# A two-block transformer kernel on Trainium2: raw tokens transposed, first weights in pieces, the second attention's norms moved, halves of features at each handover

## The reference

```python
h = rms_norm(x, norm_mix[l])                      # x * rsqrt(mean(x*x) + 1e-6), then * gain
proj = jnp.einsum('btd,de->bte', h, w_in[l])      # 1024 -> 4352
q_a, k_a, v_a, q_b, k_b, v_b, g_a, g_b = jnp.split(proj, IN_SPLITS, axis=-1)
q_a = rms_norm(q_a.reshape(B, T, NA_HEADS, HEAD_DIM), q_norm_a[l])
k_a = rms_norm(k_a.reshape(B, T, NA_HEADS, HEAD_DIM), k_norm_a[l])
o_a = neighbourhood_attention(q_a, k_a, v_a, rpb_a[l]).reshape(B, T, A_W)
q_b = rms_norm(q_b.reshape(B, T, SW_HEADS, HEAD_DIM), q_norm_b[l])
k_b = rms_norm(k_b.reshape(B, T, SW_KV_HEADS, HEAD_DIM), k_norm_b[l])
o_b = sliding_window_attention(q_b, k_b, v_b, sink_b[l], t5_table).reshape(B, T, B_QW)
y = (jax.nn.sigmoid(g_a) * jnp.einsum('bte,ed->btd', o_a, w_branch_a[l])
     + jax.nn.sigmoid(g_b) * jnp.einsum('bte,ed->btd', o_b, w_branch_b[l]))
x = x + jnp.einsum('btd,de->bte', y, w_out[l])
h = rms_norm(x, norm_ffn[l])
u = jax.nn.silu(jnp.einsum('btd,df->btf', h, w_gate[l])) * jnp.einsum('btd,df->btf', h, w_up[l])
x = x + jnp.einsum('btf,fd->btd', u, w_down[l])
```

## Time and profile before

| | |
|---|---|
| median of 3 runs | 1085.29 us (1083.16 to 1090.6) |
| the profiled execution | 1087.0 us |
| its span from first to last instruction | 1085.2 us |
| TensorE busy | 920.6 us, 85% |
| VectorE busy | 444.6 us, 41% |
| ScalarE busy | 317.4 us, 29% |
| moved by DMA | 294.90 MB, mean 272 GB/s |
| mean granted TensorE clock | 0.949 |

### The profile page before, as it was taken

How to read it: one execution, slowest core, us unless ns; L and a number is a source line. 1 busy time by engine, 2 the same in 40 slices (tenths; PEclk the granted TensorE clock), 3 DMA queues, 4 the chain that set the end, 5 groups by cost and what they waited for, 6 DMA issues and landing times.

```text
span 1085.2 us, 18086 instructions
## 1 busy us (share of the span) xinstructions
PE 920.6 (85%) x7830; PEld 653.7 (60%) x7830; DVE 444.6 (41%) x556; ACT 317.4 (29%) x400; POOL 19.0 (2%) x36
## 2 busy tenths in 40 slices
PE   5989998999999998999988978776867768677875
PEld 5989987899999888999977823131313113131311
DVE  4576778466565438995766501010101000010102
ACT  5346674273443418554433300000000000000001
POOL 1300000000000000000000100000000000000000
PEclk9998999999999999999998998898989899998988
DMA  9993244336555445352035889999999999999994
GB/s 340 263 331 106 80 155 155 122 128 209 164 179 210 160 154 212 134 195 79 4 120 199 325 347 422 420 422 422 422 422 422 422 422 422 422 422 422 422 422 174
DMA packets 83396, 294.90 MB, mean 272 GB/s; under 512 B 5888, under 2 KB 33168, under 8 KB 58625
## 3 DMA queue, kind: packets, MB, share of 16 engines
q1 hardware_dynamic: 78240, 284.18, 67.4%
q10 hardware_dynamic: 3552, 6.07, 1.6%
q0 software_dynamic: 1536, 3.68, 1.3%
HBM read 290.76 MB, written 4.10 MB: 272 GB/s over the span
## 4 chain that ended last, share of the span: by engine, by line
PE 52%; DMA 36%; DVE 6%; SPq 2%; issue 2%; ACT 2%; DVEq 0%; ACTq 0%
DMA arena<-in_w_down 19%; DMA arena<-in_w_up 16%; PE psum L929 13%; PE psum L930 13%; PE psum L931 13%; PE psum L1230 3%; PE psum L1433 3%; SPq L790 2%; DVE ring_rounded L1888 1%; PE psum L904 1%; PE psum L896 1%; PE psum L1453 1%; PE psum L1002 1%; PE psum L1422 1%; PE psum L1480 1%
## 5 line engine op out<-in xcount | busy, mean ns | idle before, releaser
L1433 PE MATMUL psum<-arena,featL 128*32 128x512 f32 x1024 | 181.1, 681 | 64.2 <-DMA arena<-in_w_up 47.5
L1888 DVE TENSOR_TENSOR ring_rounded<-arena,hi_rounded 128x2048 fp32r<-128x2048 f32 x77 | 176.0, 2289 | 96.2 <-ACT hi_rounded L1535 95.2
L1535 ACT ACTIVATE hi_rounded<-arena 128x2048 fp32r<-128x2048 f32 x77 | 146.8, 1912 | 164.6 <-PE psum L931 55.8
L929 PE MATMUL psum<-hi_rounded,featT_rounded 128*128 128x256 f32 (+1 forms) x560 | 167.6, 299 | 10.0 <-DVE featL_rounded L1911 5.4
L930 PE MATMUL psum<-ring_rounded,featT_rounded 128*128 128x256 f32 (+1 forms) x560 | 165.5, 296 | 0.0
L931 PE MATMUL psum<-hi_rounded,featL_rounded 128*128 128x256 f32 (+1 forms) x560 | 165.3, 295 | 0.0
L1433 PEld LDWEIGHTS psum<-arena,featL 128*32 128x32 f32 x1024 | 40.2, 121 | 198.4 <-DMA arena<-in_w_up 88.3
L1453 PE MATMUL psum<-arena 128*32 128x512 f32 x512 | 95.7, 673 | 45.6 <-DMA arena<-in_w_down 39.8
L929 PEld LDWEIGHTS psum<-hi_rounded,featT_rounded 128*128 128x128 f32 x560 | 111.2, 199 | 13.3 <-DVE featL_rounded L1911 6.0
L930 PEld LDWEIGHTS psum<-ring_rounded,featT_rounded 128*128 128x128 f32 x560 | 111.3, 199 | 1.2
L931 PEld LDWEIGHTS psum<-hi_rounded,featL_rounded 128*128 128x128 f32 x560 | 111.1, 198 | 1.3
(11 more groups left out here) (279 smaller groups left out, 1137.0 us busy)
## 6 DMA issues: line engine op xcount, KB each, us to landing
arena<-in_w_gate SPq DMA_DIRECT2D x75, 1024.0 KB, 26.5
arena<-in_w_up SPq DMA_DIRECT2D x75, 1024.0 KB, 26.6
arena<-in_w_down SPq DMA_DIRECT2D x65, 1024.0 KB, 26.7
arena<-in_w_in SPq DMA_DIRECT2D x14, 2048.0 KB, 8.8
arena<-in_w_down SPq DMA_DIRECT2D x5, 2048.0 KB, 7.8
arena<-in_w_out SPq DMA_DIRECT2D x4, 2048.0 KB, 8.3
arena<-in_w_in SPq DMA_DIRECT2D x4, 1024.0 KB, 9.5
t_copies<-arena ACTq DMA_DIRECT2D x1, 2048.0 KB, 7.6
```

The source lines that it names most:

```text
L929: mm(o, lhs[0], rhs[0], start=start, stop=False, skip_group_check=True)
L1433: ins = mm(psum[32 * j:32 * j + 32, MB[4 + m], :], xg[:, 4 * half + k, 32 * j:32 * j + 32], quad[quad_slot(q)][:, j, 512 * k:512 * k + 512 ...
L1535: fn(high, view, ACT.Copy).then_inc(hi_ready, 1)
L1888: tt(low, view, high.bitcast(F32), ALU.subtract).then_inc(lo_ready, 1)
```

## The change

- The tokens are transposed as they are, without the norm. The two halves of the features take turns, each with its own gain, rounding and remainder. The factor of the norm, one for each token, is applied when ScalarE empties the projections (`scaled`), which is now two instructions, one for each tile of tokens. The squares and roots come behind the roundings of chunk 0 in ScalarE's program and ahead of that of chunk 1.
- The half of the first weight unit that holds chunk 0 is loaded by four DMAs of two row blocks each, and rounded and subtracted in four pieces (`first_high`, in `norm_T` of VectorE); `first_project` waits for each piece.
- TensorE multiplies zeros ahead of and behind the first transposes (`awake`, 16 and 10 matmuls).
- The matmul of `t5` stands behind unit 3 instead of unit 2.
- Squares and sums for `qb` and `kb` stand in VectorE's step 0 behind the remainder of chunk 10, root in ScalarE's step 0, scaling in VectorE's step 1 ahead of `weighted(0)`, transposes and copies in step 2. `kdup` and the temporary lie in `xn`.
- `y`: the first half of the features is transposed and split behind each tile of the second branch, both first weight remainders of `wo` come ahead of the last two tiles, and the first chunk of `wo` is multiplied in two halves of features, the last group's transposes between them.
- `features` with `lows` does the first six row blocks for both halves of the chunk, and then the last two.

Left out below: the same moves in `plan_fills`, the definitions of semaphores, `kdup`, and the split of the norms' loop into `qk_squares` and `qk_scaled`, which hold the same instructions as before.

```diff
                     off, k, w, src = parts[0]
-                    for h in range(2):
-                        cols_ = slice(w // 2 * h, w // 2 * (h + 1))
-                        nc.sync.dma_start(piece(off, k, w)[:, :, cols_], src[:, :, cols_]).then_inc((first_in, slot_in[0])[h], 16)
+                    for j in range(4):
+                        nc.sync.dma_start(piece(off, k, w)[:, 2 * j:2 * j + 2, 0:w // 2], src[:, 2 * j:2 * j + 2, 0:w // 2])\
+                            .then_inc(first_in[j], 16)
+                    nc.sync.dma_start(piece(off, k, w)[:, :, w // 2:w], src[:, :, w // 2:w]).then_inc(slot_in[0], 16)
...
             def norm_T():
-                for t in range(NT):
-                    for h in range(2):
-                        transposes(("nt", 0, t, h), [xn[:, t, (4 * h + k) * P:(4 * h + k + 1) * P] for k in range(4)],
-                                   lambda: pe.wait_ge(xn_ready, t + 1))
+                for h in range(2):
+                    for t in range(NT):
+                        transposes(("nt", 0, t, h), [x[:, t, (4 * h + k) * P:(4 * h + k + 1) * P] for k in range(4)],
+                                   lambda: pe.wait_ge(x_in[t], 16))
...
+            def first_project():
+                b = begin("p1", 0, 0).rearrange("p (t n) -> p t n", t=NT)
+                for j in range(4):
+                    if j < 3:
+                        pe.wait_ge(first_lo, j + 1)
+                    else:
+                        wait_split(pe, 0)
+                    for t in range(NT):
+                        pe.wait_ge(feat_lo, 2 * (j // 2) + t + 1)
+                        ins = project_tile(b, 0, t, range(2 * j, 2 * j + 2), fresh=j + t == 0)
                 end(ins)
...
             def features(key, name, c, feats, lows=None):
...
                 wait_split(pe, g)
-                for f in range(2):
-                    for k in range(DK):
-                        if lows is not None and f == 0 and k % 2 == 0:
-                            pe.wait_ge(feat_lo, lows + k // 2 + 1)
-                        ins = mm3(b[:, f, :], [part(g, k, P * f, P) for part in (hi_cols, lo_cols)],
-                                  [r[:, k, :] for r in feats], k == 0, k == DK - 1)
+                for ks in (range(DK),) if lows is None else (range(0, 6), range(6, DK)):
+                    for f in range(2):
+                        for k in ks:
+                            if lows is not None and f == 0 and k % 2 == 0:
+                                pe.wait_ge(feat_lo, lows + k // 2 + 1)
+                            ins = mm3(b[:, f, :], [part(g, k, P * f, P) for part in (hi_cols, lo_cols)],
+                                      [r[:, k, :] for r in feats], k == 0 and (f == 0 or lows is None), k == DK - 1)
                 end(ins)
...
+            def awake(n):
+                for _ in range(n):
+                    mm(psum[:, 7, 0:P], rt[:, 512:512 + P], rt[:, 512:512 + P], start=True, stop=True)
+            pe.wait_ge(blank_ready, 1)
+            awake(16)
             pe.wait_ge(ident_in, 32)
             norm_T()
+            awake(10)
...
-                    project(("p1", u, c), ("p1", u), c, first=u + c == 0)
-                if u == 2:
+                    if u + c == 0:
+                        first_project()
+                    else:
+                        project(("p1", u, c), ("p1", u), c)
+                if u == 3:
...
                     scores(i)
                 if i >= 1:
                     turned(i - 1)
-                if i == 0:
-                    turn_qk("qb", "kb")
                 if i < 8:
                     u, c = 5 + i // 2, i % 2
                     project(("p1", u, c), ("p1", u), c)
+                if i == 2:
+                    turn_qk("qb", "kb")
                 if i == 8:
                     for key in ((0, 0), (0, 1), (1, 0)):
                         turn_out(*key)
                 if i >= 1:
                     weighted(i - 1)
+            def turn_y(t, h, b=None):
+                b = (begin("yT", t, h) if b is None else b).rearrange("p (k q) -> p k q", q=P)
+                pe.wait_ge(y_ready, 2 * h + t + 1)
+                for k in range(4):
+                    ins = tr(b[:, k, :], sig[:, t, (4 * h + k) * P:(4 * h + k + 1) * P], ident)
+                end(ins)
...
-            for h in range(2):
-                for t in range(NT):
-                    transposes(("yT", t, h), [sig[:, t, (4 * h + k) * P:(4 * h + k + 1) * P] for k in range(4)],
-                               lambda: pe.wait_ge(y_ready, 2 * h + t + 1))
-            wait_emptied(pe, "yT", 1, 1)
+                        if br and n:
+                            turn_y(t, 0)
+            turn_y(0, 1)
+            last_T = begin("yT", 1, 1)
+            b = begin("wo", 0, 0).rearrange("p (t n) -> p t n", t=NT)
+            g = chunk_of[("wo", 0), 0]
+            wait_split(pe, g)
+            for t in range(NT):
+                wait_emptied(pe, "yT", t, 0)
+                project_tile(b, g, t, range(DK // 2), fresh=t == 0)
+            turn_y(1, 1, last_T)
+            for t in range(NT):
+                wait_emptied(pe, "yT", t, 1)
+                ins = project_tile(b, g, t, range(DK // 2, DK), fresh=False)
+            end(ins)
...
-                fn(warm[:], eps_col[:, 0:1], ACT.Sqrt)
+                if n:
+                    fn(warm[:], eps_col[:, 0:1], ACT.Sqrt)
...
-            def high_features():
+            def high_features(h):
...
                 for t in range(NT):
-                    for h in range(2):
-                        wait_emptied(act, "nt", 0, t, h)
-                        fn(featR[:, 4 * h:4 * h + 4, t * P:(t + 1) * P],
-                           featL[:, 4 * h:4 * h + 4, t * P:(t + 1) * P], ACT.Copy).then_inc(feat_hi, 1)
+                    wait_emptied(act, "nt", 0, t, h)
+                    fn(featR[:, 4 * h:4 * h + 4, t * P:(t + 1) * P],
+                       featL[:, 4 * h:4 * h + 4, t * P:(t + 1) * P], ACT.Copy).then_inc(feat_hi, 1)
...
+            def first_high(j):
+                high, view, _ = hi_view(0)
+                act.wait_ge(first_in[j], 16)
+                fn(high[:, 2 * j:2 * j + 2], view[:, 2 * j:2 * j + 2], ACT.Copy).then_inc(first_hi if j < 3 else hi_ready, 1)
...
             act.wait_ge(eps_ready, 3)
+            fn(warm[:], eps_col[:, 0:1], ACT.Sqrt)
+            high_features(0)
+            for j in range(2):
+                first_high(j)
+            high_features(1)
+            for j in range(2, 4):
+                first_high(j)
             squares(0, lambda t: act.wait_ge(x_in[t], 16))
-            high_part(0)
-            high_features()
             high_part(1)
...
+            def scaled(dst, lo, u, c):
+                b = bank("p1", u, c).rearrange("p (t n) -> p t n", t=NT)
+                a.link(fn(dst[:, 0, lo:lo + 256], b[:, 0, :], ACT.Copy, scale=st[:, 0:1]))
+                empty(fn(dst[:, 1, lo:lo + 256], b[:, 1, :], ACT.Copy, scale=st[:, 1:2]), "p1", u, c)
             act.wait_ge(ident_in, 32)
+            act.wait_ge(scale0_ready, NT)
...
-                empty(fn(nat[:, :, lo:lo + 256], bank("p1", u, c).rearrange("p (t n) -> p t n", t=NT), ACT.Copy), "p1", u, c)
-                if n == 5:
+                scaled(nat, lo, u, c)
+                if n == 7:
                     wait_filled(act, "t5")
...
-            root(*QK_SUMS[1], HD, 0)
...
-                if i == 0:
-                    qk_moved("qb", "kb")
...
-                    ins = fn(sig[:, :, 256 * i:256 * i + 256], bank("p1", u, c).rearrange("p (t n) -> p t n", t=NT), ACT.Copy)
-                    empty(ins, "p1", u, c)
+                    scaled(sig, 256 * i, u, c)
                     high_part(first["p1", 5] + i + 2)
+                    if i == 0:
+                        root(*QK_SUMS[1], HD, 0)
+                    if i == 2:
+                        qk_moved("qb", "kb")
...
+                _, whole, rounded = hi_view(0)
+                high0 = hi_view(0)[0]
+                for h in range(2):
+                    for t in range(NT):
+                        wait_filled(dve, "nt", 0, t, h)
+                        gain = bc(colp("norm0")[:, 4 * h:4 * h + 4], P)
+                        empty(tt(view(featL, t, h), bank("nt", 0, t, h).rearrange("p (k q) -> p k q", k=4), gain, ALU.mult),
+                              "nt", 0, t, h)
+                    for t in range(NT):
+                        highs[0] += 1
+                        dve.wait_ge(feat_hi, highs[0])
+                        tt(view(featLR, t, h), view(featL, t, h), view(featR, t, h).bitcast(F32), ALU.subtract).then_inc(feat_lo, 1)
+                    for j in (2 * h, 2 * h + 1):
+                        ks = slice(2 * j, 2 * j + 2)
+                        if j < 3:
+                            dve.wait_ge(first_hi, j + 1)
+                        else:
+                            dve.wait_ge(hi_ready, 1)
```

(28 more changed lines are left out.)

93 lines of the change are left out of this document (41 added, 52 removed).

## The result

| | before | after |
|---|---|---|
| median | 1085.79 us (1083.13 to 1090.8, 20 runs) | 1091.36 us (1087.56 to 1094.82, 20 runs) |
| span of the profiled execution | 1085.2 us | 1090.0 us |

The ratio is 1.0047, with a 95% interval of 1.0033 to 1.0061: the change makes the kernel about 5 us slower. That is inside the forecast range (1082.5 to 1094.0) and 2.5 us above the predicted 1088.9.

What follows compares the result with a forecast made beforehand. Before 225 us TensorE's waits, mostly for VectorE's operands, shift everything behind them, with no slack. Start and bias matmul +3.5, Part 4 +4.4, Part 5 -4.3 give +3.6: 1088.9 us on the median, range 1082.5 to 1094.0.

Steps and rivals of the forecast that it cites:

- Part 1: Start, first projection chunks: TensorE waits ahead of chunks 1 and 2, and chunk 2 ends 5.1 us later.
- Rival (a): Start: the DMA issues run through once delayed, chunk 2 starts at 29.4; net -0.9, 1084.4 us; chance 0.28.
- rival (b): Waits of 3.9, 4.0, 1.6 and 4.3 us go with their echoes: up to -16, 1069 to 1075 us; chance 0.06.
- Fillers: Zero matmuls ahead of the first transposes: the 16 end at 6.5 us, 1.8 us of harm kept for the range.
- Part 2: Second attention's bias matmul, one unit later: its wait for the last parameter transfer goes, 1.6 us gained.
- Part 3: Scaled copies, 17 evacuations as two instructions each: hidden in ScalarE's free time, at most 0.8 us in all.
- Part 4: Second attention's norms later: new wait of 5.4 us ahead of the first weighted product; 4.4 us worse, bounds 2.4 to 6.4.
- Part 5: Halves at the handovers: 4.3 us gained at the second branch, bounds 3 and 6.1; nothing at feed-forward and second block.
- Rival (c): After each of three new waits TensorE's next chunk runs wholly at the lower clock; about 1097 us; chance 0.08.

Runs made afterwards that it cites:

- start_fixed: Changed kernel with the eight DMA issues behind the roundings of chunks 2 and 3 and chunk 1's rounding ahead of the squares, on ScalarE only: 1087.53 us.
- issues_late: Changed kernel with the eight DMA issues of the constants behind the roundings of chunks 2 and 3: 1088.29 us.
- start_both: start_fixed plus VectorE's remainder of chunk 1 ahead of its two reciprocals: 1083.18 us.
- round1_first: Changed kernel with ScalarE's rounding of chunk 1 ahead of the squares, DMA issues still behind both: 1091.93 us.
- best_no_fill: best without the 26 filler matmuls around the first transposes: 1071.11 us.
- best: Changed kernel with the edits of start_both and att_new together: 1070.01 us.
- t5_back: Changed kernel with the second attention's bias matmul back behind the third unit, its copy and store two chunks earlier: 1092.81 us.
- norms_back: Changed kernel with squares, root, scaling and transposes of the second attention back where the kernel before has them: 1088.37 us.
- y_only: Kernel before with only the halves at the handovers (y transposed and split in halves, first output chunk in halves): 1081.06 us.
- pairs_only: Kernel before with each of its 17 copies out of the projections' banks split into two instructions, without the scale: 1086.67 us.
- start_norms: start_both with the second attention's norms and transposes back where the kernel before has them: 1079.49 us.
- att_new: Changed kernel with VectorE's and ScalarE's order around the first attention step changed: roundings of chunks 9 and 10 earlier, norm work moved: 1079.5 us.

## Why the prediction was right

**Start (Part 1).** Said: wait of 4 ahead of chunk 1, which starts at 21.7; chunk 2 at 32.0, its end 5.1 late. Measured: 3.44, 21.72, 32.73, and an end 5.8 late (40.2, from 32.73 and 7.5, against 34.4, from 40.20, where the first four chunks ended before, less 5.75). The choice that carried it was to let the block of issues shift at its full 10.6 us; it took 11.1, with the one issue of 5.34 in it. Rival (a), that the issues run through, is false: in every kernel the lora issue takes 4.7 to 5.4 us, wherever it stands between 15.6 and 22.6. The length of the block is no constant, though: over all kernels it was 8.8 (start_fixed) to 11.1 us, and what sets it was not found. The four pieces of chunk 0's weights cost nothing, as said: ScalarE rounds them at 9.74 and 13.66, each pair right behind the features, without a wait for a transfer. What holds chunk 2 is shown by issues_late, what holds chunk 1 by the pair start_fixed and start_both. The prediction named only ScalarE's squares, and for the kernel it was about that is enough; that VectorE's reciprocals would take over as soon as ScalarE's order is mended (round1_first) it did not see, and its rival (b) asks for ScalarE's order alone.

**Fillers.** I let the 16 first ones end at 6.5 and kept 1.8 us of harm; they end at 7.2, 0.4 after the inputs are in by best_no_fill. In the other kernels they end between 6.3 and 7.7, by when the clock rises: their records, two to a filler, start every 0.21 us before that and every 0.11 after it. Chunk 0 nonetheless is through at 18.3, as against 17.7 forecast, and it sets nothing, since chunk 1 stands behind it. In best, where it could, they are worth 0.3 us at the end of chunk 7 and nothing that the medians show.

**Bias matmul (Part 2).** The balance at the end of chunk 8 was right, +4.1 for +3.5, but the 1.6 us was put down to the wrong cause. The last parameter transfer takes less time in the changed kernel:

```profile
wr<-in_wr ACTq DMA_DIRECT2D x1, 144.0 KB, 18.2
```

Issued at 27.42, it lands near 45.6; before it took 31.0 and landed at 53.3. The matmul would not have waited in its old place, as t5_back shows: moving it is worth nothing. I had assumed that the landing could only be as late or later.

**Copies in two (Part 3).** Nothing, within 0.0 to 2.4, as said.

**Attention (Part 4).** Said: from the end of chunk 8 to that of the second weighted product 39.1 us in place of 34.7. Measured: 39.1 (77.72 to 116.80). The path over VectorE was exact: with E the end of chunk 8, the weighted product starts at E+25.25, and E+25.3 was said. Three other parts were less so, and cancel. TensorE was ready at E+20.8 and not E+19.9, because chunk 9 started at E+4.5 and took 8.4; so the new wait was 4.4, not 5.4. The low clock behind it cost 2.5, not 2.0 (weighted product 1.97, scores 2.08, transposes 1.77 in place of 1.1 each). The moved transposes took 1.3, not 1.8. norms_back puts the whole of it at 3.7 us by the ratios and 4.2 by the trace. The 34.7 it is compared with is itself one execution's: in y_only and pairs_only chunk 9 ran in 5.99 us, chunk 10 then waited 1.3, and the same stretch took 33.9 and 34.1.

By the Trainium skill, TensorE: Matmul & The Clock Gate, Part 4, the transposes would have kept the clock low about 1 us longer than the 2.0. It was 0.5 longer, and chunk 11, right behind them, took 5.99, all at full clock, so this trace doesn't tell the two apart. Two others do, and against the page. In pairs_only TensorE idles 4.19 us ahead of the twelve transposes of queries and keys:

```profile
78.50 2.79 PE L904 MATMUL psum<-cst,arena 128*128 128x128 f32 x12 [4.19 <-DVE arena L1953]
81.98 0.35 PE L929 MATMUL psum<-hi_rounded,featT_rounded 128*128 128x256 f32 x1 [0.68 <-DVE ring_rounded L1891]
```

From 78.1 to 81.4 the granted clock is 0.50, and the transposes are all that TensorE does there; from 81.5 to 88 it is 1.00, and chunk 9 takes 5.99. In y_only it goes the same way (0.50 from 78.3 to 81.6, then 1.00). So the clock came back with nothing but transposes since it fell. Behind the same transposes chunk 9 took 8.4 in the kernel before, 8.1 in norms_back and 7.9 in start_norms. The prediction read the 8.4 as agreeing with the page; it is one of two outcomes, and the other contradicts it.

Not foreseen at all were two table loads on ScalarE, since the root now stands between exponentials:

```profile
93.67 1.28 ACT L1569 ACT_TABLE_LOAD   x1
94.97 0.31 ACT L1569 ACTIVATE st<-st 128x20 f32<-128x20 f32 x1
...
96.40 1.28 ACT L1691 ACT_TABLE_LOAD   x1 [0.64 <-DVE st L2058]
```

They cost nothing here, because VectorE's queue and not ScalarE sets the wait; I had counted the root as one short instruction.

**Handovers (Part 5).** 4.3 said; 4.0 in the changed kernel (38.3 us instead of 42.2 from the last step of the attention to the end of output chunk 1), 4.2 in y_only.

**Sum and rivals.** +3.6 said; by the same places +4.55. Of the difference of 1.0, Part 1 has 0.7 and Part 5 0.3. The wrong cause in Part 2 and the three sizes in Part 4 do not show in the sum; that they cost it nothing is luck. Rival (c), a clock that doesn't come back, is false: chunk 1 takes 7.5 us, not 10.3. Rival (b) was mis-added (its waits and echoes come to 19.8, not 16), but it is the one worth keeping: the change doesn't do what it says because each engine works through one fixed order, and with that order put right it gives what (b) promised. best has 1070.0 where (b) gave 1069 to 1075.

## What to carry to other kernels

When a piece of work is moved on one engine, look at every engine's fixed order for what it now stands ahead of: here two squares with their roots (2.8 us in all), then two reciprocals of 0.16, and eight DMA issues each held back a matrix chunk by 3.5 us. A shift of work pays when its new place is where the engine idled; the same norms cost 3.7 us more in one late place and, spread over idle stretches with the roundings brought forward, went with a gain of 12, of which the roundings have a part that was not measured. A change that gives nothing may hold a good part and two bad orders: take its parts one at a time, and where mending one engine's order hands the wait to another's, mend both before judging.

## What the runs showed of the hardware

**A lower clock can come after the wait has ended, and may miss the chunk behind it.** In the changed kernel chunk 1 starts at 21.72 after 3.44 us of idling, and its first matmuls still start every 0.12 us:

```profile
22.78 0.28 PE L937 MATMUL psum<-hi_rounded,featL_rounded 128*128 128x256 f32 x1
22.90 0.33 PE L935 MATMUL psum<-hi_rounded,featT_rounded 128*128 128x256 f32 x1
...
23.46 0.41 PE L935 MATMUL psum<-hi_rounded,featT_rounded 128*128 128x256 f32 x1
23.67 0.41 PE L936 MATMUL psum<-ring_rounded,featT_rounded 128*128 128x256 f32 x1
...
26.43 0.28 PE L937 MATMUL psum<-hi_rounded,featL_rounded 128*128 128x256 f32 x1
```

From 23.0 to 26.4 they start every 0.21 us (the level of 1.2 GHz), then every 0.12 again (2.4 GHz). It took 7.5 us in all, as in round1_first and start_fixed. In norms_back, issues_late, att_new and t5_back the same chunk behind the same wait ran wholly at the full clock (6.0 us). Chunk 9 behind 3.5 us took 8.4 in the changed kernel, up to 8.7 in three others (8.70 in round1_first), 7.5 in start_fixed and 7.4 in start_both. So a wait's echo, the time that the work behind it loses at the lower clock, lies between 0 and 2.7 us (8.7 less 6.0) in that chunk, and the 2.0 that I took is no constant. Nor does the longest wait have the largest: behind 5.34 us in start_both the weighted product and the scores lost 1.3. A chunk spared can pay elsewhere: in norms_back, att_new and t5_back chunk 2 then waited 4.7, 4.4 and 4.6 instead of 3.5, since VectorE set its start, and took 8.0 to 8.2 instead of 7.5.

**One execution tells the early part well and the total poorly.** The distance from the kernel before, in us (at 225 us, at 617, at the end of the span): changed kernel +4.6, +6.5, +4.8; issues_late -1.7, +0.5, +1.6; att_new -7.1, -2.4, -4.4; y_only -5.2, -8.2, -7.0. The code behind 225 us is all but the same in them. From 540 to 600 us the granted clock was 0.89 in the changed kernel, 0.83 in att_new, 0.97 in pairs_only and 0.91 in the kernel before. For most kernels the medians agree with the distance at 225 us: against the changed kernel att_new is 11.7 ahead there and 12.4 by the ratios, best 20.8 and 20.4, norms_back 3.8 and 3.7. Not so for issues_late (6.2 and 3.5), start_fixed (6.5 and 4.6), start_both (10.8 and 8.1) and start_norms (13.5 and 10.1). All four have the eight issues behind the roundings, but so has best, which gives hardly anything back; why these four do was not found.
